# Adding up the norm sums on GpSimd, and the low parts in the three-operand form, in a four-layer model kernel

## The chip, the core and the metric

The kernel runs on one core of one Trainium2 chip, in one launch. The metric is the device time of the program in microseconds, the median of three runs before the change. A time difference of a few microseconds is a difference of a tenth of a per cent here.

## The reference, cut to what matters

A token stream of 256 tokens with 2048 features passes two layers of a first model (token mixer, then MLP, each with adaptive modulation) and two layers of a second one (an S5 layer and a FoX attention layer). Around the change only the end of each of the six branches matters:

```
y = branch(h)                                  # last step: a product with a 2048-wide weight
x = x + gate * rms_norm(y, g_post)             # for each branch
h = rms_norm(x, g_pre) * (1 + scale) + shift   # the next branch's input
```

`rms_norm` divides by the root of the mean over the 2048 features of a token. Everything is held in 32-bit floats, and products must be about that exact.

## The kernel before, in words

**Layout and slabs.** Activations lie with features on the 128 partitions: 16 blocks of 128 features by 256 tokens. Every large weight comes as slabs of 2048 x 128 (1 MB), one after the other through five buffers RAW that SyncE fills in a fixed order (`load`, L2455). One slab gives one block of 128 output features. There are 507 slabs; `slab` (L409) does 32 matmuls with each.

**High and low parts.** TensorE takes a rounded 32-bit format (fp32r). So ScalarE rounds a slab to its high part WH (`high`, L890), VectorE takes the rest WL = RAW - WH (`low`, L1566, whole slabs; `low_part`, L1562, halves of a slab), and the activations are held as high and low part beside each other. TensorE does 16 matmuls of 512 columns with WH (against high and low part), then waits for WL and does 16 of 256 columns with it. WH and WL have two buffers each. `low` counts `s_free`, on which TensorE waits before the second half and on which SyncE waits before it fills the RAW buffer again. Some slabs are used unsplit.

**Turns.** The last 16 slabs of a branch are a "turn"; there are six, i = 0 to 5 (output projection and last quarter of the down projection of layer 0: i = 0, 1; of layer 1: i = 2, 3; S5 output: i = 4; FoX output: i = 5). For output block n of a turn VectorE adds the halves of the PSUM bank to a block YT (`joined`, L1545; in turns 1 and 3 one more addition), multiplies it with the gate and x (`y_times_x`, L1634), and ScalarE squares it twice (`y_parts`, L943). These three results stand side by side in one of three buffers TS (3 x 256 columns). `y_add` (L1653) adds TS of block n to the running sum TACC. In turn 5 only the first 256 columns are there. TensorE later sums TACC and the last block's TS over the partitions with a matmul of ones (`y_sums`, L504), which waits for 14 additions of the turn. From these sums come the norm of y and that of the new x.

**Order on VectorE.** In `y_slab` (L1665) VectorE does, for each slab n of a turn: `y_times_x` of block n - 1, `y_add` of block n - 2, and `next_low` (L1574): first the modulation tile if there is one after this slab (`tile`, L1580), then the low part of the slab after. A modulation tile is 1 MB of another weight that VectorE multiplies with a broadcast row and sums; in turn 0 nearly every slab has one. In turn 3 VectorE also builds tables for the S5 layer between the slabs (names aq and abt).

**Waits on the sum.** With n >= 4, ScalarE and VectorE wait for the addition of block n - 3 before they write block n to TS again, since TS has three buffers. The engines run their instructions in the order in which the program issues them. GpSimd does nothing but four small fills at the start.

All two-operand instructions of VectorE are issued by one helper (`tt`, line L1535 in the rows), the three-operand ones by another (`stt`, L1543), matmuls by L403, ScalarE's by L888.

Of the kernel before, what the change touches and what calls it, by code (L numbers as in the profile page):

```python
# [6 lines left out]
F32 = mybir.dt.float32  # L7
F32R = mybir.dt.float32r
ALU = mybir.AluOpType
# [8 lines left out]
RING = 5  # L18
# [88 lines left out]
POS, TILE_POS, OUT_POS, LOADS = {}, {}, [], []  # L107
# [62 lines left out]
def build(nc, d, out):  # L170
    ctx = ExitStack()
    with ctx:
# [4 lines left out]
        def at(name, shape, off, dt=F32):  # L177
            return nc.alloc_sbuf_tensor_at(name, (P, *shape), dt, offset=off)
# [4 lines left out]
        def sem(name):  # L183
            return ctx.enter_context(nc.semaphore(name))
# [4 lines left out]
        RAW = [at(f"raw{i}", (KT, 128), o + 8 * kb * i) for i in range(RING)]; o += 8 * kb * RING  # L189
        WH = [at(f"wh{i}", (KT, 128), o + 8 * kb * i, F32R) for i in range(2)]; o += 16 * kb  # L190
        WL = [at(f"wl{i}", (KT, 128), o + 8 * kb * i, F32R) for i in range(2)]; o += 16 * kb
# [33 lines left out]
        TACC = at("tacc", (3, T), A0)  # L225
        TS = [at(f"ts{i}", (3, T), A0 + 3 * kb * (i + 1)) for i in range(3)]
# [95 lines left out]
        s_free = sem("s_free")  # L322
# [10 lines left out]
        s_ysq, s_yg, s_y2 = sem("s_ysq"), sem("s_yg"), sem("s_y2")  # L333
        s_t1, s_yadd = sem("s_t1"), sem("s_yadd")
# [1191 lines left out]
        def vector(e):  # L1526
# [7 lines left out]
            def tt(o_, a_, b_, op):  # L1534
                return e.tensor_tensor(o_, a_, b_, op)  # L1535
# [25 lines left out]

            def low_part(j, q):  # L1562
                w = PLACE_OF[j]
                return tt(WL[w][:, q, :], RAW[POS[j] % RING][:, q, :], WH[w][:, q, :].bitcast(F32), ALU.subtract)

            def low(j):  # L1566
                if j >= N_SLABS:
                    return
                e.wait_ge(s_hi, HI_AT[j])
                w = PLACE_OF[j]  # L1570
                tt(WL[w][:, :, :], RAW[POS[j] % RING][:, :, :], WH[w][:, :, :].bitcast(F32),
                   ALU.subtract).then_inc(s_free, 1)

            def next_low(j):  # L1574
                for t in TILES_AFTER.get(j, []):
                    tile(t)
                if j in SPLIT:
                    low(SPLIT[j])
# [55 lines left out]
            def y_times_x(i, n):  # L1634

                if i == 5:
                    return
                if i in (1, 3):
                    e.wait_ge(s_yt, 24 * (i - 1) + 32 + n + 1)
                else:  # L1640
                    e.wait_ge(s_ev, TURNS[i] + n + 1)
                if n >= 4:
                    e.wait_ge(s_yadd, 14 * i + n - 3)
                stt((TS[n % 3] if n else TACC)[:, 1, :], YT[n % 2][:, :], gate(i)[:, n:n + 1], X[:, n, :], ALU.mult,
                    ALU.mult).then_inc(s_t1, 1)
# [4 lines left out]
                    return modulation(i // 2, GATE_M if i % 2 else GATE_A)  # L1650
                return PRM[:, S5_POST:S5_POST + 16]

            def y_add(i, n):  # L1653

                q = slice(0, 1 if i == 5 else 3)
                if i == 5:
                    e.wait_ge(s_yg, 16 * i + n + 1)
                else:
                    e.wait_ge(s_y2, 16 * i + n + 1)
                    e.wait_ge(s_t1, 16 * i + n + 1)  # L1660
                if n >= 2:
                    e.wait_ge(s_yadd, 14 * i + n - 1)
                tt(TACC[:, q, :], TACC[:, q, :], TS[n % 3][:, q, :], ALU.add).then_inc(s_yadd, 1)

            def y_slab(i, n):  # L1665

                if n:
                    y_times_x(i, n - 1)
                if n >= 3:
                    y_add(i, n - 2)  # L1670
                next_low(TURNS[i] + n)
                if n == 15:
                    y_add(i, 14)

            def x_new(i, taken=None):
                y_times_x(i, 15)
# [3 lines left out]
                if i < 5:  # L1680
                    e.wait_ge(s_hi, HI_AT[TURNS[i] + 19])
                    low_part(TURNS[i] + 19, slice(0, 8))
# [33 lines left out]
                if i < 5:  # L1716
                    low_part(TURNS[i] + 19, slice(8, 16)).then_inc(s_free, 1)
                    for c in range(4):
                        normed(c)
                    for c in range(4):  # L1720
                        h_chunk_low(i, c)
                        if c == 1:
                            taken()
# [365 lines left out]
            def layer(l):  # L2089
# [17 lines left out]
                for n in range(16):  # L2107
                    if n == 0:
                        mixer_joined(l, N_IN - 1)
                        m_gated(l, 3)  # L2110
                        m_low(l, 3)
                    else:
                        joined(J_OUT[l] + n - 1, YT[(n - 1) % 2][:, :])
                    y_slab(2 * l, n)
                joined(J_OUT[l] + 15, YT[1][:, :])
                x_new(2 * l, lambda: up_taken(l, 0))
                for j in range(4):
                    for n in range(16):
                        if n:
                            up_squared(l, j, n - 1)  # L2120
                        elif j:
                            down_joined(l, j - 1, 15)
                        if n >= 2:
                            up_low(l, j, n - 2)
                        next_low(up_slab(l, j, n))
                        if l == 1:
                            s5_parameters(32 * j + n)
                    for n in range(16):
                        if n == 0:
                            up_squared(l, j, 15)  # L2130
                            up_low(l, j, 14)
                            up_low(l, j, 15)
                        else:
                            down_joined(l, j, n - 1)
                        if j == 3:
                            y_slab(2 * l + 1, n)
                        else:
                            next_low(down_slab(l, j, n))
                        if l == 1:
                            s5_parameters(32 * j + 16 + n)  # L2140
# [82 lines left out]
            def third():  # L2223
# [52 lines left out]
                for n in range(16):  # L2276
                    if n == 0:
                        joined(J_GLU + 15, ZF[1][:, :])
                        glu_gated(14)
                        glu_low(14)  # L2280
                        glu_gated(15)
                        glu_low(15)
                    else:
                        joined(J_Y2 + n - 1, YT[(n - 1) % 2][:, :], 0.25)
                    y_slab(4, n)
# [119 lines left out]
            for b in range(4):  # L2405
                e.wait_ge(s_ct0, b + 1)
                q = slice(512 * b, 512 * b + 512)
# [20 lines left out]
            for l in range(2):  # L2428
                s0 = PER_LAYER * l + SINK
                settled(ts(MINUS_SINKS[:, 16 * l:16 * l + 16], PRM[:, s0:s0 + 16], -1.0, None, ALU.mult))  # L2430
            h_chunk_low(-1, 3)
            low(RAMP)
            low(RAMP + 1)
            layer(0)
            layer(1)
            third()
            fourth()


        def source(j):  # L2440
            for l in range(2):
                if j < J_OUT[l]:
                    return d["w_in"][l, j - J_IN[l]]
                if j < J_MLP[l]:
                    return d["w_out"][l, j - J_OUT[l]]
                if j < J_MLP[l] + 128:
                    part, n = divmod(j - J_MLP[l], 32)
                    return d["w_up"][l, 16 * part + n] if n < 16 else d["w_down"][l, 16 * part + n - 16]
            for first, name in ((J_Y3, "fox_w_out"), (J_FOX, "fox_w_in"), (J_KV, "kv_w"), (J_Y2, "s5_w_out"),
                                (J_GLU, "s5_w_glu"), (J_U, "s5_w_in")):  # L2450
                if j >= first:
                    return d[name][j - first]
# [62 lines left out]
        with nc.Block() as block:  # L2515
            @block.sync
            def _(e):
                sync(e)

            @block.scalar  # L2520
            def _(e):
                scalar(e)

            @block.vector
            def _(e):
                vector(e)

            @block.tensor
            def _(e):
                tensor(e)  # L2530
# [132 lines left out]
```

## Time and profile before

| | us |
|---|---|
| median of three runs | 3237.44 (3228.82 to 3237.97) |
| the profiled execution | 3234.48 |
| its span | 3232.6 |
| TensorE busy | 3096.2 (96%) |
| VectorE busy | 2518.7 (78%) |
| ScalarE busy | 1567.5 (48%) |
| GpSimd busy | 0.2 |
| mean DMA rate | 244 GB/s |

Turn 0 lies at about 361 to 450 us of the span, turn 1 at 1087 to 1168, turn 2 at 1435 to 1518, turn 3 at 2180 to 2262, turn 4 at 2641 to 2723, turn 5 at 3134 to 3215. The busy share of the whole is an average: an engine that is 78% busy over the span can be busy all of the time in one stage and hold TensorE up there, and that is read from a stage's own rows.

In the rows, PE is TensorE, DVE is VectorE, ACT is ScalarE, POOL is GpSimd. An instruction's duration can reach a little into its successor's, so the time that one takes in a row of many is the distance between two starts, up to 0.09 us less than its duration.

### The profile page before, as it was taken

The numbers are of one execution on the slowest core, as the hardware profiler recorded it, in microseconds if no ns is written. First come the engines' busy times: TensorE is split into PE (matmuls) and PEld (weight loads), VectorE is DVE, ScalarE is ACT, GpSimd is POOL, SyncE is SP. The second block draws the span as 40 slices with busy tenths as digits, with TensorE's granted clock in tenths as the row PEclk, the third lists the DMA queues.
The fourth block names the chain that finished last, engine by engine and source line by source line (L and its number), as shares of the span: only waits on it lengthen the run. The fifth ranks groups of instructions, "written<-read, shape, count | busy, mean of one in ns | idle before, by whom it ended". The sixth has DMA issues, their size and how long they took to land. (4 is left out here: it accounts for less than half of the span.)

```text
span 3232.6 us, 49521 instructions
## 1 busy us (share of the span) xinstructions
PE 3096.2 (96%) x20336; PEld 2691.0 (83%) x20336; DVE 2518.7 (78%) x3174; ACT 1567.5 (48%) x2348; POOL 0.2 (0%) x4
## 2 busy tenths in 40 slices
PE   4899999999999999999999999999998899999998
PEld 3788778888888888888888888888887788888887
DVE  7997999798988888777987666789669677656765
ACT  2455654444444566765534444445443456434454
POOL 0000000000000000000000000000000000000000
PEclk7999999999999999999999999999999999999999
DMA  9777869988888645554687666776554553654453
GB/s 409 303 302 302 320 248 343 336 336 332 340 331 336 237 181 208 207 220 146 248 315 264 238 206 227 262 268 239 217 174 170 181 184 135 227 185 157 145 190 109
DMA packets 136978, 790.27 MB, mean 244 GB/s; under 512 B 20081, under 2 KB 38897, under 8 KB 46001
## 3 DMA queue, kind: packets, MB, share of 16 engines
q1 hardware_dynamic: 108002, 754.65, 63.2%
q10 hardware_dynamic: 28752, 32.45, 3.1%
q8 instruction: 163, 2.67, 0.3%
q14 instruction: 61, 0.50, 0.0%
HBM read 769.28 MB, written 17.76 MB: 243 GB/s over the span
## 5 line engine op out<-in xcount | busy, mean ns | idle before, releaser
L1535 DVE TENSOR_TENSOR wl<-raw,wh 128x2048 fp32r<-128x2048 f32 (+1 forms) x484 | 1097.4, 2267 | 235.0 <-ACT wh L888 234.5
L403 PE MATMUL bk<-HX,wh 128*128 128x512 f32 x4592 | 1117.1, 396 | 4.5 <-ACT wh L888 3.0
L403 PEld LDWEIGHTS bk<-HX,wh 128*128 128x128 f32 x4592 | 845.5, 189 | 178.5 <-ACT wh L888 3.6
L888 ACT ACTIVATE wh<-raw 128x2048 fp32r<-128x2048 f32 x479 | 913.7, 1908 | 31.8 <-DMA raw<-in_w_in 26.1
L403 PEld LDWEIGHTS bk<-HX,wl 128*128 128x128 f32 x4592 | 571.2, 188 | 31.3 <-DVE wl L1535 8.8
L403 PE MATMUL bk<-HX,wl 128*128 128x256 f32 x4592 | 579.1, 278 | 3.7 <-DVE wl L1535 3.7
L403 PE MATMUL bk<-hb,wh 128*128 128x512 f32 x2048 | 492.1, 392 | 2.7 <-ACT hb L888 2.4
L1543 DVE SCALAR_TENSOR_TENSOR raw<-raw,cb 128x2048 f32<-128x2048 f32 x192 | 437.5, 2285 | 14.9 <-DMA raw<-in_w_ada 14.9
L403 PEld LDWEIGHTS bk<-hb,wh 128*128 128x128 f32 x2048 | 375.3, 188 | 78.5 <-ACT hb L888 3.2
L403 PEld LDWEIGHTS bk<-hb,wl 128*128 128x128 f32 x2048 | 256.4, 189 | 12.1 <-DVE wl L1535 1.6
L403 PE MATMUL bk<-hb,wl 128*128 128x256 f32 x2048 | 259.1, 279 | 0.8 <-DVE wl L1535 0.8
L888 ACT ACTIVATE yt<-bk 128x256 f32<-128x256 f32 x160 | 61.3, 383 | 366.4 <-PE bk L403 366.4
L888 ACT ACTIVATE ur<-bk 128x256 f32<-128x256 f32 x122 | 46.8, 384 | 368.6 <-PE bk L403 361.6
L403 PE MATMUL bk<-sq,raw 128*128 128x257 f32 (+1 forms) x544 | 119.5, 380 | 2.3 <-ACT sq L888 2.3
L403 PEld LDWEIGHTS bk<-sq,raw 128*128 128x128 f32 x544 | 102.4, 189 | 18.8 <-issue 4.2
L1535 DVE TENSOR_TENSOR y<-bk,y 128x256 f32<-128x256 f32 x96 | 40.7, 424 | 75.8 <-ACT yt L888 51.7
L1535 DVE TENSOR_TENSOR ur<-bk,ur 128x256 f32<-128x256 f32 x122 | 51.3, 421 | 60.5 <-ACT ur L888 60.1
L403 PE MATMUL bk<-hf,rampw 128*128 128x256 f32 x192 | 48.3, 416 | 49.2 <-DMA rampw<-in_w_in 41.1
L403 PEld LDWEIGHTS bk<-hf,rampw 128*128 128x128 f32 x192 | 39.9, 211 | 57.5 <-DMA rampw<-in_w_in 26.0
L1535 DVE TENSOR_TENSOR tacc<-tacc,ts 128x768 f32<-128x768 f32 (+1 forms) x84 | 72.5, 863 | 1.2 <-ACT yu L888 0.6
L403 PE MATMUL bk<-ax,wh 128*128 128x512 f32 x256 | 64.8, 395 | 6.2 <-ACT wh L888 6.2
L403 PE MATMUL bk<-mx,wh 128*128 128x512 f32 x256 | 65.3, 396 | 1.2 <-DVE mx L1535 1.2
(299 smaller groups left out, 2706.1 us busy)
## 6 DMA issues: line engine op xcount, KB each, us to landing
raw<-in_w_ada SPq DMA_DIRECT2D x192, 1024.0 KB, 5.8
raw<-in_w_up SPq DMA_DIRECT2D x128, 1024.0 KB, 5.6
raw<-in_w_down SPq DMA_DIRECT2D x128, 1024.0 KB, 5.2
raw<-in_w_in SPq DMA_DIRECT2D x68, 1024.0 KB, 5.3
raw<-in_kv_w SPq DMA_DIRECT2D x33, 1024.0 KB, 4.8
raw<-in_w_out SPq DMA_DIRECT2D x32, 1024.0 KB, 4.8
raw<-in_s_w_in SPq DMA_DIRECT2D x32, 1024.0 KB, 4.8
raw<-in_fox_w_in SPq DMA_DIRECT2D x32, 1024.0 KB, 4.8
```

The source lines that it names most:

```text
L403: return e.matmul(o_, l_, r_, start=start, stop=stop, skip_group_check=True)
L888: return e.activation(o_, i_, f, **kw)
L1535: return e.tensor_tensor(o_, a_, b_, op)
L1543: return e.scalar_tensor_tensor(o_, a_, s_, b_, op0, op1, accum_out=sums)
```

## The change

The function `y_add` leaves VectorE and is issued on GpSimd, as GpSimd's only work in the program: 84 additions (14 in each of six turns; 768 columns in turns 0 to 4, 256 in turn 5), each with the same waits as before. VectorE's `y_slab` no longer has them. And every low part, which was a two-operand subtraction RAW - WH, is a three-operand instruction (RAW * 1.0) - WH: 474 whole slabs and ten halves.

```diff
             def low_part(j, q):
                 w = PLACE_OF[j]
-                return tt(WL[w][:, q, :], RAW[POS[j] % RING][:, q, :], WH[w][:, q, :].bitcast(F32), ALU.subtract)
+                return stt(WL[w][:, q, :], RAW[POS[j] % RING][:, q, :], 1.0, WH[w][:, q, :].bitcast(F32), ALU.mult,
+                           ALU.subtract)
...
-                tt(WL[w][:, :, :], RAW[POS[j] % RING][:, :, :], WH[w][:, :, :].bitcast(F32),
-                   ALU.subtract).then_inc(s_free, 1)
+                stt(WL[w][:, :, :], RAW[POS[j] % RING][:, :, :], 1.0, WH[w][:, :, :].bitcast(F32), ALU.mult,
+                    ALU.subtract).then_inc(s_free, 1)
...
             def y_slab(i, n):
 
                 if n:
                     y_times_x(i, n - 1)
-                if n >= 3:
-                    y_add(i, n - 2)
                 next_low(TURNS[i] + n)
-                if n == 15:
-                    y_add(i, 14)
...
+        def gpsimd(e):
+
+            def y_add(i, n):
+
+                q = slice(0, 1 if i == 5 else 3)
+                if i == 5:
+                    e.wait_ge(s_yg, 16 * i + n + 1)
+                else:
+                    e.wait_ge(s_y2, 16 * i + n + 1)
+                    e.wait_ge(s_t1, 16 * i + n + 1)
+                if n >= 2:
+                    e.wait_ge(s_yadd, 14 * i + n - 1)
+                e.tensor_tensor(TACC[:, q, :], TACC[:, q, :], TS[n % 3][:, q, :], ALU.add).then_inc(s_yadd, 1)
+
+            for i in range(6):
+                for n in range(1, 15):
+                    y_add(i, n)
```

On VectorE, in turn 0, two slabs stood like this before (ts is a block's three results, raw with cb a modulation tile, wl the low part, yt the block's halves joined):

```order
L1535 TENSOR_TENSOR tacc<-tacc,ts_87 128x768
L1543 SCALAR_TENSOR_TENSOR raw_54,mod<-raw_54,cb 128x2048
L1535 TENSOR_TENSOR wl_58<-raw_50,wh_56 128x2048
L1535 TENSOR_TENSOR yt_149<-bk,yt_149 128x256
L1543 SCALAR_TENSOR_TENSOR ts_86<-yt_149,mod,X 128x256
L1535 TENSOR_TENSOR tacc<-tacc,ts_88 128x768
```

and the same place now (with the buffers' numbers):

```order
L1543 SCALAR_TENSOR_TENSOR raw4_54,mod_61<-raw4_54,cb_69 128x2048
L1543 SCALAR_TENSOR_TENSOR wl1_58<-raw0_50,wh1_56 128x2048
L1535 TENSOR_TENSOR yt1_149<-bk1,yt1_149 128x256
L1543 SCALAR_TENSOR_TENSOR ts0_86<-yt1_149,mod_61,X_49 128x256
L1543 SCALAR_TENSOR_TENSOR raw1_51,mod_61<-raw1_51,cb_69 128x2048
```

The addition is gone from the row, and the low part has changed its form; nothing else has moved. GpSimd has, from the start of turn 0:

```order
L2437 TENSOR_TENSOR tacc<-tacc,ts_87 128x768 [waits s_t1,s_y2]
L2437 TENSOR_TENSOR tacc<-tacc,ts_88 128x768 [waits s_yadd,s_t1,s_y2]
L2437 TENSOR_TENSOR tacc<-tacc,ts_86 128x768 [waits s_yadd,s_t1,s_y2]
L2437 TENSOR_TENSOR tacc<-tacc,ts_87 128x768 [waits s_yadd,s_t1,s_y2]
L2437 TENSOR_TENSOR tacc<-tacc,ts_88 128x768 [waits s_yadd,s_t1,s_y2]
```

Each addition waits there for the block's product and second square, and for the addition before it; it no longer stands in front of a tile or a low part.

## Rows read from the trace of the kernel before

**Rows 1.** The page's first part: busy time, share of the span, instructions.

```profile
PE 3096.2 (96%) x20336; PEld 2691.0 (83%) x20336; DVE 2518.7 (78%) x3174; ACT 1567.5 (48%) x2348; POOL 0.2 (0%) x4
```

**Rows 2.** Waits of TensorE in turn 0, then in turn 3: total, times, longest.

```profile
PE bk L403 <- DVE wl L1535: 3.1, 9, 0.6
...
PE bk L403 <- DVE wl L1535: 0.8, 2, 0.5
```

**Rows 3.** TensorE in time order, turn 0: start, duration, what, idle before it.

```profile
366.94 2.00 PE L403 MATMUL bk<-ax,wh 128*128 128x512 f32 x8
...
383.52 2.00 PE L403 MATMUL bk<-ax,wh 128*128 128x512 f32 x8
...
444.94 2.00 PE L403 MATMUL bk<-ax,wh 128*128 128x512 f32 x8
...
450.50 1.45 PE L403 MATMUL bk<-tacc,ones 128*128 128x256 f32 x4
```

**Rows 4.** VectorE in time order, turn 0.

```profile
365.33 2.28 DVE L1543 SCALAR_TENSOR_TENSOR raw<-raw,cb 128x2048 f32<-128x2048 f32 x1
...
370.60 2.29 DVE L1543 SCALAR_TENSOR_TENSOR raw<-raw,cb 128x2048 f32<-128x2048 f32 x1
...
375.87 0.95 DVE L1535 TENSOR_TENSOR tacc<-tacc,ts 128x768 f32<-128x768 f32 x1
...
400.42 0.95 DVE L1535 TENSOR_TENSOR tacc<-tacc,ts 128x768 f32<-128x768 f32 x1
401.29 2.29 DVE L1543 SCALAR_TENSOR_TENSOR raw<-raw,cb 128x2048 f32<-128x2048 f32 x1
403.50 0.08 DVE L1543 DVE_READ_ACCUMULATOR raw<-raw,cb 128x1 f32 x1
...
443.66 0.95 DVE L1535 TENSOR_TENSOR tacc<-tacc,ts 128x768 f32<-128x768 f32 x1
...
447.59 2.04 DVE L1535 TENSOR_TENSOR tacc<-tacc,ts 128x768 f32<-128x768 f32 x2
```

**Rows 5.** ScalarE in time order, turn 0: the second square of a block.

```profile
400.34 0.49 ACT L888 ACTIVATE ts<-yt,mod 128x256 f32<-128x256 f32 x1
```

**Rows 6.** Windows: length, PE, PEld, DVE, ACT, POOL, clock, DMA share, GB/s.

```profile
40.00:90.00 50.00, 22.73 (x93) 18.90 (x93) 37.19 (x44) 3.97 (x8) 0.00 (x0) 0.73 1.01 421
...
387.30:442.90 55.60, 52.48 (x289) 43.31 (x288) 55.25 (x57) 32.28 (x46) 0.00 (x0) 1.00 0.90 343
```

**Rows 7.** TensorE in time order, turn 2.

```profile
1440.70 1.99 PE L403 MATMUL bk<-ax,wh 128*128 128x512 f32 x8
...
1451.73 1.99 PE L403 MATMUL bk<-ax,wh 128*128 128x512 f32 x8
...
1517.93 1.45 PE L403 MATMUL bk<-tacc,ones 128*128 128x256 f32 x4
```

**Rows 8.** VectorE in time order, turn 2, its last block before the sums.

```profile
1513.14 0.42 DVE L1535 TENSOR_TENSOR yt<-bk,yt 128x256 f32<-128x256 f32 x1 [1.45 <-ACT yt L888]
1513.60 0.48 DVE L1543 SCALAR_TENSOR_TENSOR ts<-yt,mod,X 128x256 f32<-128x256 f32 x1
```

**Rows 9.** VectorE in time order, turn 3.

```profile
2185.23 0.42 DVE L1535 TENSOR_TENSOR yt<-bk,yt 128x256 f32<-128x256 f32 x1
...
2233.46 0.42 DVE L1535 TENSOR_TENSOR yt<-bk,yt 128x256 f32<-128x256 f32 x1
```

**Rows 10.** All waits of VectorE in turn 3.

```profile
DVE yt L1535 <- ACT yt L888: 4.1, 6, 1.3
```

**Rows 11.** VectorE's groups by shape: form, count, busy us, mean ns, idle before.

```profile
L1535 DVE TENSOR_TENSOR wl<-raw,wh 128x2048 fp32r<-128x2048 f32 x474 | 1085.2, 2290 | 235.0 <-ACT wh L888 234.5
L1543 DVE SCALAR_TENSOR_TENSOR raw<-raw,cb 128x2048 f32<-128x2048 f32 x192 | 437.5, 2285 | 14.9 <-DMA raw<-in_w_ada 14.9
...
L1543 DVE SCALAR_TENSOR_TENSOR ts<-yt,mod,X 128x256 f32<-128x256 f32 x60 | 29.1, 485 | 2.3 <-DVE yt L1535 0.2
...
L1543 DVE SCALAR_TENSOR_TENSOR zz<-fe,zz 128x256 f32<-128x256 f32 x16 | 6.7, 420 | 0.5 <-ACT fe L888 0.5
```

More of the change, by code:

```diff
@@ L1651, in gate @@
                 return PRM[:, S5_POST:S5_POST + 16]
[L1653 to L1663, printed above, removed]
             def y_slab(i, n):
@@ L2526, in _ @@
                 vector(e)
+            @block.gpsimd
+            def _(e):
+                gpsimd(e)
             @block.tensor
```

## The prediction, made blind

> **What bounds the kernel now.** I began with the page's busy shares [rows 1]: TensorE is busy 96% of the span, VectorE 78%, GpSimd not at all. So time can fall only where TensorE runs slower than it could, and an engine with 78% on average may well be full in some stage. The change touches the six turns, so I then asked for TensorE's waits in each turn. In turns 1, 2, 4 and 5 it waits for nothing; in turn 0 it waits for the low part nine times, 3.1 us in sum, in turn 3 twice, 0.8 us [rows 2].
>
> The sum of the waits is not what turn 0 loses. Look at the pace in the time order [rows 3, 7]. Ten slabs go from 383.52 to 444.94, which is 6.14 us each. The three before them go from 366.94 to 383.52, 5.53 us each, and in turn 2, with the same shapes, two slabs take 1440.70 to 1451.73, 5.52 us each. So TensorE's own pace is 5.53 us and it runs at 6.14. (The matmuls after each wait are stretched, so part of the loss is in no wait.)
>
> VectorE's time order shows why [rows 4]. In turn 0 its rows follow each other without a gap: product, addition, modulation tile, low part, joined block. Before the additions begin one round takes 365.33 to 370.60, 5.27 us. The addition takes 400.42 to 401.29, 0.87 us on the path. Together 6.14 us, which is exactly TensorE's pace: turn 0 is bound by VectorE, at its throughput. In turn 2 the tile is missing and VectorE waits 1.45 us per slab for ScalarE [rows 8].
>
> **What the change removes.** 84 additions leave VectorE, 70 of them of 768 columns and 0.95 us [rows 4]. In turn 0 that takes VectorE's round from 6.14 to 5.27 us, under TensorE's 5.53. TensorE becomes the bound there: ten slabs take 10 x 5.53 = 55.3 instead of 61.4 us, a gain of 6.1 us. It is not 12 x 0.87 = 10.4 us (twelve additions, the first and the last in [rows 4], precede the last low part), because TensorE's own pace takes over at 5.53. What is late next is nothing of VectorE, which then has 0.26 us per slab to spare.
>
> In turn 3 the S5 tables fill VectorE: eight slabs from 2185.23 to 2233.46, 6.03 us each [rows 9], against TensorE's 5.53. The lag is mostly eaten by slack and surfaces as the 0.8 us of [rows 2]; without the additions it doesn't build up. Gain 0.8 us. In turns 1, 2, 4 and 5 the addition lies beside TensorE's work and its going is worth nothing. There the cover is VectorE's wait for ScalarE, 1.45 us per slab in turn 2.
>
> **What it adds: the additions on GpSimd.** The trace shows no such instruction. From below it could be as short as VectorE's 0.95 us, from above I take one slab, 5.53 us, where the chain of additions would itself become the bound; the value is nearer to VectorE's row, between 1 and 2 us. With no contention this is worth nothing anywhere: one addition per slab, and a block's buffer is used again three blocks later. The only hard edge is the end of a turn, where TensorE's sum waits for the 14th addition. In turn 2 the last product starts at 1513.60 and ends 0.48 us later [rows 8], and TensorE comes to the sum at 1517.93 [rows 7]: 3.8 us are there. In turn 0 the last two additions start on VectorE at 447.59 and the sum comes at 450.50 [rows 3, 4], 2.9 us for the last alone, since GpSimd does the one before it a slab earlier; and there VectorE's late joining falls away too. An addition of up to 2.5 us is covered. Cost 0, at most a few tenths per turn.
>
> **The form of the low part.** A three-operand instruction over the same 2048 columns with two inputs in SBUF takes 2285 ns, the two-operand low part 2290 [rows 11]. The tile also sums up and has a further row of 0.08 us for it [rows 4], which the low part will not have. A per-partition scalar costs something (485 against 420 ns at 256 columns [rows 11]), but here the scalar is a constant. So the cost is zero; from above 474 x 0.065 = 31 us of VectorE's busy time, of which even in turn 0 0.065 us per slab would be covered by the 0.26 to spare. From below, 5 ns per slab are nothing.
> The Trainium skill, Vector Engine (DVE) Microarchitecture Reference, section "Points that are easy to get wrong", says that this form with two SBUF sources that are not bf16 halves throughput. By that each low part would take about twice its time and the change would be a clear loss. The row of the tile, two 32-bit sources in SBUF and 2285 ns, says otherwise, and the row decides.
>
> **Transfers.** In turn 0 each slab needs two transfers of 1 MB. At 6.14 us that is 342 GB/s, and the row has 343 at a DMA share of 0.90 [rows 6]. At 5.53 us it must be 379, a share of 0.90 x 6.14 / 5.53 = 1.00. At the start of the program the queues moved 421 GB/s [rows 6], so it just fits; I count 0, at worst the 6.1 us don't come.
>
> **Sum.** 6.1 + 0.8 = 6.9 us. The profiled execution took 3234.5 us (span 3232.6), which gives 3227.6; the median of the runs is 3 us above that execution, so by the median 3230.5, and I say 3231.
>
> **Rivals.** *The shared port (slower).* If GpSimd and VectorE can't both read SBUF with two-input instructions at a time, VectorE stands still while GpSimd adds. The addition becomes ready when ScalarE's second square ends at 400.83 [rows 5], when VectorE is already in the tile from 401.29 or, without the addition, from 400.42 [rows 4], and VectorE's row in turn 0 has no gap to give. With an addition of P us VectorE's round is 5.27 + P: it is slower than before from P = 0.87 us on, and the full 6.1 us come only if P is under 0.26. For P = 1.4 turn 0 costs 12 x 0.53 = 6.4 us more than before; turn 3 has eleven additions there, 5.8 us, less VectorE's 4.1 us of waits [rows 10], 1.7; in sum +8, 3245.5. For P = 1.9 it is 12.4 + 11.3 - 4.1 = +19.6, 3257. I take 3250. For it: VectorE's rows follow on each other so densely that GpSimd must collide with something. Against it: the trace has no row of GpSimd at work, so nothing shows that either engine is held; and a form at full speed with two inputs leaves open how they are read.
> The Trainium skill, SBUF — State Buffer, section "Who interferes with whom", states just this rule: a VectorE instruction with two SBUF inputs contends with a GpSimd instruction that reads SBUF, and whoever comes second is blocked. It names no exception for the three-operand form. The GPSIMD Engine Reference, section "Elementwise — side-by-side cycle accounting", has GpSimd's addition 1.96 times as long as VectorE's, an estimate of P of about 1.9 us. No run here shows either yet.
>
> *The bound passes on (no gain).* VectorE is free but the transfers hold turn 0 at 343 GB/s, or ScalarE's chain square, rounding, copy does. Then only turn 3's 0.8 us come: 3236.6. For it the DMA share of 0.90, against it the 421 GB/s at the start.
>
> **How the numbers follow.** The forecast (no contention, 6.9 us gained) has a chance of 0.42, its own range 3226 to 3236 because the runs before spread over 9 us. The shared port has 0.38, the passed-on bound, with small mixtures near zero, 0.20. About 0.3% (9.7 us) is what a measurement tells from no change. Faster than that (under 3227.7) is only the low edge of the forecast, 0.08. Slower (over 3247.1) is the larger part of the shared port, 0.28. The rest, 0.64, is no change. The range 3226 to 3252 holds all but the top of the shared port and the lowest edge.
>
> **What the profile after would show.** Right: TensorE's slabs in turn 0 every 5.53 us, no wait for the low part there, VectorE with gaps of about 0.26 us, DMA near 379 GB/s, GpSimd's additions under 2.5 us and no VectorE row longer than before. The shared port: low parts, tiles or products in the turns longer than 2290, 2285 and 485 ns, or late after a free predecessor, in all six turns, and a pace in turn 0 over 6.14 us. The passed-on bound: ScalarE's rounding waiting for transfers, and a pace near 6.1. Wrong altogether would be low parts that are longer outside the turns, where GpSimd does nothing.

## The result, and the profile after

The changed kernel takes 3247.4 us (median of seven runs, 3244.14 to 3251.66) against 3237.44 us in as many runs of the kernel before (3228.82 to 3244.57). The ratio is 1.0036 with a 95% interval of 1.0021 to 1.0051: slower by 0.36%, which is 12 us (the two medians lie 10 us apart), where I had forecast 7 us faster. The forecast was wrong; the rival of the shared port said 3245 to 3257.

The profiled execution has a span of 3249.8 us. Its page gives GpSimd work to do, and it is more than was taken from VectorE:

```profile
PE 3103.3 (95%) x20336; PEld 2695.1 (83%) x20336; DVE 2489.4 (77%) x3090; ACT 1568.4 (48%) x2348; POOL 249.4 (8%) x88
```

VectorE is rid of 84 additions but only of 29 us of busy time against [rows 1], not of the 72.5 us that these took on it. Instructions that became longer take back 35 us; the remaining 8 us or so are no work at all, since a duration reaches a little into its successor's and is counted there once. The groups by shape tell which became longer (line, form, count, busy us, mean ns, idle before):

```profile
L1543 DVE SCALAR_TENSOR_TENSOR wl<-raw,wh 128x2048 fp32r<-128x2048 f32 x474 | 1103.5, 2328 | 265.3 <-ACT wh L888 264.6
L1543 DVE SCALAR_TENSOR_TENSOR raw<-raw,cb 128x2048 f32<-128x2048 f32 x192 | 437.4, 2285 | 13.9 <-DMA raw<-in_w_ada 13.8
...
L1535 DVE TENSOR_TENSOR aq<-ah,bq 128x768 f32<-128x768 f32 x32 | 35.8, 1160 | 1.3 <-DMA ah<-at_keep 1.3
...
L1535 DVE TENSOR_TENSOR yt<-y,yt 128x256 f32<-128x256 f32 x32 | 21.6, 675 | 1.1
```

The low parts have grown by 18 us, one addition of blocks (yt<-y,yt) by 8 us and the table products (aq) by 7 us; two single instructions of turn 0 make up the other 2 us. A mean of 2328 ns instead of 2290 looks like a small, even slowing. It is not. In time order it is eleven instructions of 3.94 us, all in turn 0, and 463 that are as before (11 x 1.65 us is the whole difference of 18 us). Two slabs of turn 0 on VectorE, then the same stretch on GpSimd:

```profile
391.98 0.48 DVE L1543 SCALAR_TENSOR_TENSOR ts<-yt,mod,X 128x256 f32<-128x256 f32 x1
392.38 2.28 DVE L1543 SCALAR_TENSOR_TENSOR raw<-raw,cb 128x2048 f32<-128x2048 f32 x1
394.59 0.08 DVE L1543 DVE_READ_ACCUMULATOR raw<-raw,cb 128x1 f32 x1
394.59 3.94 DVE L1543 SCALAR_TENSOR_TENSOR wl<-raw,wh 128x2048 fp32r<-128x2048 f32 x1
398.46 0.41 DVE L1535 TENSOR_TENSOR yt<-bk,yt 128x256 f32<-128x256 f32 x1
398.90 0.48 DVE L1543 SCALAR_TENSOR_TENSOR ts<-yt,mod,X 128x256 f32<-128x256 f32 x1
399.31 2.28 DVE L1543 SCALAR_TENSOR_TENSOR raw<-raw,cb 128x2048 f32<-128x2048 f32 x1
401.52 0.08 DVE L1543 DVE_READ_ACCUMULATOR raw<-raw,cb 128x1 f32 x1
401.52 3.94 DVE L1543 SCALAR_TENSOR_TENSOR wl<-raw,wh 128x2048 fp32r<-128x2048 f32 x1
```

```profile
392.88 3.51 POOL L2437 TENSOR_TENSOR tacc<-tacc,ts 128x768 f32<-128x768 f32 x1 [3.42 <-ACT ts L888]
399.80 3.50 POOL L2437 TENSOR_TENSOR tacc<-tacc,ts 128x768 f32<-128x768 f32 x1 [3.42 <-ACT ts L888]
...
459.21 1.86 POOL L2437 TENSOR_TENSOR tacc<-tacc,ts 128x768 f32<-128x768 f32 x1 [0.42 <-DVE ts L1543]
```

Read the two together. The addition becomes ready at 392.88, while VectorE is in a tile. It cannot do its work at once: it takes 3.5 us, where the last of the turn, with VectorE idle beside it, takes 1.86. The 1.7 us that are left to the tile's end at 394.59 are its wait, which the trace counts as its duration. Then the addition has the port, and now the low part stands still: it takes 3.94 us instead of 2.29, 1.65 us more. Each instruction that waits looks busy; in these rows a stall at the port shows as a long instruction, never as idle time.

VectorE's round is now 399.31 - 392.38 = 6.93 us, against 5.27 + 0.87 = 6.14 before [rows 4], and TensorE follows it (start, duration, what, idle before):

```profile
393.66 2.00 PE L403 MATMUL bk<-ax,wh 128*128 128x512 f32 x8
395.49 2.00 PE L403 MATMUL bk<-mx,wh 128*128 128x512 f32 x8
398.59 1.21 PE L403 MATMUL bk<-ax,wl 128*128 128x256 f32 x8 [1.10 <-DVE wl L1543]
399.64 1.10 PE L403 MATMUL bk<-mx,wl 128*128 128x256 f32 x8
400.58 2.00 PE L403 MATMUL bk<-ax,wh 128*128 128x512 f32 x8
```

Its waits for the low part in turn 0 went from the 3.1 us of [rows 2] to this:

```profile
PE bk L403 <- DVE wl L1543: 12.8, 12, 1.2
```

To compare turns, take the time from the start of block 0's product on VectorE (of its square on ScalarE in turn 5) to TensorE's sum of TACC. It is the same to 0.1 us where nothing changes, in turns 1, 4 and 5. Turn 2 has 80.3 to 81.7 us in all kernels, whatever they do there. Turn 3 has 82.2 to 85.1 us in the five kernels whose turn 3 is that of before (before and four of the experiments below). In us:

| | turn 0 | turn 1 | turn 2 | turn 3 | turn 4 | turn 5 |
|---|---|---|---|---|---|---|
| before | 85.57 | 81.19 | 80.68 | 82.21 | 81.10 | 80.51 |
| changed | 95.69 | 81.18 | 81.70 | 86.45 | 81.10 | 80.50 |

Turn 0 costs 10.1 us. Turn 3 shows 4.2 us in this pair, but the three kernels with whole additions on GpSimd there have 86.0 to 86.5 us against the 82.2 to 85.1, so its own loss is known only as 1 to 4 us. Together that is 11 to 14 us, inside the interval of the ratio (7 to 17 us). The 17 us between the two profiled spans contain 3 us from stretches that the change doesn't touch.

Turn 3 shows the other side of the same thing. VectorE, then GpSimd:

```profile
2218.72 0.42 DVE L1535 TENSOR_TENSOR yt<-bk,yt 128x256 f32<-128x256 f32 x1 [0.91 <-ACT yt L888]
2219.18 1.06 DVE L1535 TENSOR_TENSOR yt<-y,yt 128x256 f32<-128x256 f32 x1
...
2220.68 2.28 DVE L1543 SCALAR_TENSOR_TENSOR wl<-raw,wh 128x2048 fp32r<-128x2048 f32 x1
2222.88 3.48 DVE L1535 TENSOR_TENSOR aq<-ah,bq 128x768 f32<-128x768 f32 x2
```

```profile
2218.10 1.86 POOL L2437 TENSOR_TENSOR tacc<-tacc,ts 128x768 f32<-128x768 f32 x1 [6.55 <-ACT ts L888]
2221.28 3.41 POOL L2437 TENSOR_TENSOR tacc<-tacc,ts 128x768 f32<-128x768 f32 x1 [1.32 <-ACT ts L888]
```

From 2218.10 to 2219.96 GpSimd adds. The joining of a block, with one input in PSUM and one in SBUF, runs in the middle of it at its usual 0.42 us. The next instruction has both inputs in SBUF and takes 1.06 instead of 0.43 us; it ends 0.28 us after the addition. The next addition becomes ready at 2221.28, in the low part, and waits for its end; then the pair of table products takes 3.48 instead of 1.82 us, again 1.66 more. Later in the turn, where no table products follow, the stall is 1.2 us (1.62 instead of 0.42 us, four times), since the joining hides a part of the addition.

In turns 1, 2, 4 and 5 no instruction of VectorE is longer. There GpSimd is the one that waits: in turn 2 an addition starts at 1468.44, in the low part from 1467.70 to 1469.99, and takes 3.27 us; it then works while VectorE waits for ScalarE.

### The profile page after: what moved, and what is told of

It is laid out like the page before. It is cut to its first block and busy times, and to the rows that moved or that the text cites. A ratio compares the mean times of both kernels' runs of the same rounds, so it can differ in the third digit from the quotient of the medians.

```text
span 3249.8 us, 49523 instructions
## 1 busy us (share of the span) xinstructions
PE 3103.3 (95%) x20336; PEld 2695.1 (83%) x20336; DVE 2489.4 (77%) x3090; ACT 1568.4 (48%) x2348; POOL 249.4 (8%) x88
## 5 line engine op out<-in xcount | busy, mean ns | idle before, releaser
L1543 DVE SCALAR_TENSOR_TENSOR wl<-raw,wh 128x2048 fp32r<-128x2048 f32 (+1 forms) x484 | 1115.7, 2305 | 265.3 <-ACT wh L888 264.6
L2437 POOL TENSOR_TENSOR tacc<-tacc,ts 128x768 f32<-128x768 f32 (+1 forms) x84 | 249.2, 2966 | 2980.2 <-ACT ts L888 2517.1
L1535 DVE TENSOR_TENSOR yt<-bk,yt 128x256 f32<-128x256 f32 x64 | 26.9, 421 | 61.7 <-ACT yt L888 61.7
```

Of the source, the lines that this page charges most:

```text
L1543: return e.scalar_tensor_tensor(o_, a_, s_, b_, op0, op1, accum_out=sums)
L2437: e.tensor_tensor(TACC[:, q, :], TACC[:, q, :], TS[n % 3][:, q, :], ALU.add).then_inc(s_yadd, 1)
```

## The experiments

The theory after these rows is that a GpSimd instruction that reads SBUF and a VectorE instruction with two inputs in SBUF exclude each other for whole instructions, and that the one that waits gets the port when the other's instruction ends. The rivals are that the three-operand form is to blame, that the loss sits in later sums at the turns' ends, or that something other than VectorE holds turn 0.

**form_only.** The three-operand low parts alone, with the additions left on VectorE.

```diff
-                tt(WL[w][:, :, :], RAW[...][:, :, :], WH[w][:, :, :].bitcast(F32), ALU.subtract)
+                stt(WL[w][:, :, :], RAW[...][:, :, :], 1.0, WH[w][:, :, :].bitcast(F32), ALU.mult, ALU.subtract)
```

> The low parts in the three-operand form, the additions left on VectorE. Theory (GpSimd's additions and VectorE's two-input instructions exclude each other, whatever the form): no change, ratio 1.000, whole low parts 2.29 us everywhere, turn 0 at 6.14 us per slab. Rival (the three-operand form is what costs): the whole loss is here, about +11 us, low parts longer than 2.29 us.

Ratio 0.9996 (0.9987 to 1.0005), turn 0 85.57 us:

```profile
L1543 DVE SCALAR_TENSOR_TENSOR wl<-raw,wh 128x2048 fp32r<-128x2048 f32 x474 | 1085.1, 2289 | 234.4 <-ACT wh L888 234.0
```

2289 against 2290 ns [rows 11]: the form by itself costs nothing, and does not lose half its rate.

**gp_two_operand.** The additions alone on GpSimd: the changed kernel with the low parts' `stt` put back to `tt`.

> The additions on GpSimd, the low parts in the old two-operand form. Theory: as the changed kernel, ratio about 1.0036 (1.002 to 1.005), low parts in turn 0 about 3.94 us and its slabs 6.93 us apart. Rival one (the three-operand form is the one that collides): 3230 us, low parts 2.29 us, turn 0 at 5.53 us. Rival two (the two-operand form collides worse, which the change wanted to avoid): slower than the changed kernel, above 3250 us, with low parts over 3.94 us or low parts of other turns lengthened too.

Ratio 1.0032 (1.0020 to 1.0045), turn 0 95.68 us, turn 3 86.14. In turn 0:

```profile
400.94 3.94 DVE L1535 TENSOR_TENSOR wl<-raw,wh 128x2048 fp32r<-128x2048 f32 x1
```

The same 3.94 us in both forms. The two-operand form collides neither more nor less, so the three-operand form buys nothing. Both rivals about the form fall.

**no_add.** GpSimd's instruction is kept with all its waits, but cut to one column; the sums are left out:

```diff
-                e.tensor_tensor(TACC[:, q, :], TACC[:, q, :], TS[n % 3][:, q, :], ALU.add).then_inc(s_yadd, 1)
+                e.tensor_tensor(TACC[:, 0, 0:1], TACC[:, 0, 0:1], TS[n % 3][:, 0, 0:1], ALU.add).then_inc(s_yadd, 1)
```

> Each GpSimd addition is cut to one column of one of its three parts, with all its waits and counts; the running sums are left out. Theory: with the additions' time on the shared port gone, VectorE's round in turn 0 is 5.27 us and TensorE's pace of 5.53 us takes over; turn 0 gains 6.1 us and turn 3 0.8 us over before, 3230 us, ratio 0.998, low parts 2.29 us. Rival (the bound passes on to the transfers, 343 GB/s in turn 0): 3236.6 us, turn 0 stays near 6.1 us per slab, ScalarE's rounding waits for transfers.

Ratio 0.9978 (0.9969 to 0.9987), 7 us faster than before. Turn 0 takes 79.17 us, 6.4 less than before. Stretch 390 to 440 us (length, PE, PEld, DVE, ACT, POOL busy, clock, DMA share, GB/s):

```profile
390.00:440.00 50.00, 50.00 (x291) 43.99 (x290) 46.16 (x46) 32.56 (x50) 10.42 (x10) 1.00 0.99 397
```

TensorE is full and the queues follow to a share of 0.99. So the part of the prediction that reads turn 0 as bound by VectorE, and prices its relief at 6.1 us, was right, and the rival of the passed-on bound falls. (GpSimd's 10.42 us there are ten tiny instructions of 0.2 to 2.3 us, most of which end with the tile or low part in which they become ready; the low parts keep their 2.29 us.)

**write_only.** The addition becomes a fill of the same columns, a write without a read; the sums are left out.

```diff
-                e.tensor_tensor(TACC[:, q, :], TACC[:, q, :], TS[n % 3][:, q, :], ALU.add).then_inc(s_yadd, 1)
+                e.memset(TACC[:, q, :], 1.0).then_inc(s_yadd, 1)
```

> Each GpSimd addition is replaced by a fill of the same 768 or 256 columns (a write with no read); the running sums are left out. If only reads exclude each other: low parts 2.29 us, turn 0 at 5.53 us, 3230 us. If any access of GpSimd to SBUF does: low parts in turn 0 longer by the fill's duration and a pace of 5.27 us plus that.

Ratio 0.9984 (0.9974 to 0.9994), turn 0 79.17 us, low parts 2289 ns. A fill in the middle of a tile, GpSimd and then VectorE:

```profile
403.44 0.74 POOL L2437 MEMSET tacc<- 128x768 f32 x1 [4.21 <-ACT ts L888]
```

```profile
401.99 2.29 DVE L1543 SCALAR_TENSOR_TENSOR raw<-raw,cb 128x2048 f32<-128x2048 f32 x1
```

Neither is longer: all fills of GpSimd take 0.74 us in the mean. So a write alone does not exclude, and the read does.

**one_input.** A copy of TS into TACC instead of the addition: one read. The sums are left out.

```diff
-                e.tensor_tensor(TACC[:, q, :], TACC[:, q, :], TS[n % 3][:, q, :], ALU.add).then_inc(s_yadd, 1)
+                e.tensor_copy(TACC[:, q, :], TS[n % 3][:, q, :]).then_inc(s_yadd, 1)
```

> Each GpSimd addition is replaced by a copy of the block's three results into the running sum, one input instead of two; the running sums are left out. If any read of GpSimd excludes VectorE's two-input instructions: low parts in turn 0 lengthened by about the copy's own duration, say 0.7 to 1.3 us, a pace of 6.0 to 6.6 us, 3228 to 3240 us, about the time of before. If only two-input reads do: low parts 2.29 us, pace 5.53 us, ratio 0.998.

Ratio 0.9992 (0.9982 to 1.0001). In turn 0, then GpSimd's copies there and the last one, which has no VectorE beside it:

```profile
402.59 2.90 DVE L1543 SCALAR_TENSOR_TENSOR wl<-raw,wh 128x2048 fp32r<-128x2048 f32 x1
```

```profile
400.86 2.50 POOL L2437 COPY tacc<-ts 128x768 f32<-128x768 f32 x1 [3.39 <-ACT ts L888]
...
445.54 0.83 POOL L2437 COPY tacc<-ts 128x768 f32<-128x768 f32 x1 [0.91 <-ACT ts L888]
```

One read excludes as well. The stall is 0.61 us for a copy of 0.83 us, just under my range of 0.7 to 1.3. Rounds come every 5.88 us, which is 5.27 + 0.61 and just under my 6.0 to 6.6, and turn 0 takes 83.12 us, 2.45 less than before: this stall is on the gaining side of 0.87 us. (A copy is less work than the addition, so this shows where the break-even lies, not a way to get the sums. In the time of the whole kernel it can't be told from no change.)

**gp_quiet and gp_full.** The additions of only some turns on GpSimd, the others on VectorE.

```diff
+ON_GPSIMD = (1, 2, 4, 5)        # gp_full: (0, 3)
...
+                if n >= 3 and i not in ON_GPSIMD:
+                    y_add(i, n - 2)
...
-            for i in range(6):
+            for i in ON_GPSIMD:
```

> As the changed kernel, but the additions of turns 0 and 3 are back on VectorE; 56 additions stay on GpSimd, in turns 1, 2, 4 and 5. Theory (the port stalls cost time only where VectorE has no slack, turns 0 and 3): as before, ratio 1.000 within 0.001, turn 0 at 6.14 us per slab. Rival (the loss is spread over all turns, or sits in the waits for later sums at their ends): ratio 1.002 or more.

> The counterpart: only the 28 additions of turns 0 and 3 on GpSimd. Theory: the whole loss, ratio 1.0036 (1.002 to 1.005): 10 us in turn 0 at 6.93 us per slab, 4 us in turn 3. Rival (loss spread over all turns): a third of it, ratio 1.0012.

gp_quiet: 0.9998 (0.9990 to 1.0007), turns 1, 2, 4, 5 as before. gp_full: 1.0039 (1.0026 to 1.0051), turn 0 95.66, turn 3 86.04. The 28 additions of turns 0 and 3 are the whole loss; the 56 others, 161 us of GpSimd's time, cost nothing and bring nothing. In gp_quiet GpSimd alone is held up: its additions take 3.16 us in the mean, and no VectorE instruction of the turns is longer. No run has the additions of turn 0 alone on GpSimd, so what turn 3 adds is not separated from its scatter.

**gp_split.** Each addition in three pieces of 256 columns.

```diff
-                e.tensor_tensor(TACC[:, q, :], TACC[:, q, :], TS[n % 3][:, q, :], ALU.add).then_inc(s_yadd, 1)
+                for c in range(q.stop):
+                    last = e.tensor_tensor(TACC[:, c, :], TACC[:, c, :], TS[n % 3][:, c, :], ALU.add)
+                last.then_inc(s_yadd, 1)
```

> The changed kernel, with each GpSimd addition of 768 columns issued as three of 256 (0.74 us each when alone, against 1.86 us). Theory (the port is held for a whole instruction and handed over at its end to whoever waits): every stall of VectorE becomes short, 0.5 us or so, and there are more of them: the low part about 2.8 us instead of 3.94, the product or the tile lengthened as well, and one piece partly hidden behind the joining of a block, which has one input in SBUF; turn 0 at 6.4 to 6.8 us per slab, between before (6.14) and the changed kernel (6.93), ratio about 1.002. Rival (access is shared element by element, and only the amount counts): low parts stay near 3.94 us and the pace at 6.93.

Ratio 1.0018 (1.0009 to 1.0027), turn 0 89.19 us, turn 3 85.35. One round of VectorE:

```profile
399.80 0.41 DVE L1535 TENSOR_TENSOR yt<-bk,yt 128x256 f32<-128x256 f32 x1
400.25 0.51 DVE L1543 SCALAR_TENSOR_TENSOR ts<-yt,mod,X 128x256 f32<-128x256 f32 x1
400.67 2.83 DVE L1543 SCALAR_TENSOR_TENSOR raw<-raw,cb 128x2048 f32<-128x2048 f32 x1
403.43 0.08 DVE L1543 DVE_READ_ACCUMULATOR raw<-raw,cb 128x1 f32 x1
403.43 2.82 DVE L1543 SCALAR_TENSOR_TENSOR wl<-raw,wh 128x2048 fp32r<-128x2048 f32 x1
406.17 0.41 DVE L1535 TENSOR_TENSOR yt<-bk,yt 128x256 f32<-128x256 f32 x1
```

There are three short handovers instead of one long one: tile and low part each stand still for 0.54 us, and the third piece is hidden behind the joining and leaves 0.03 us on the product. The round is 6.37 us. The port passes from one engine to the other at the end of every instruction, not element by element. In pieces the total stall is less (1.1 us against 1.65), because one piece falls where VectorE does not need the port. It still loses against 0.87 us on VectorE itself.

**pe_share and pe_three.** If neither VectorE nor GpSimd is to add, TensorE can: some of turn 0's blocks are summed over the partitions at once, into the two banks in which the sums end.

```diff
+BY_TENSOR = (3, 6, 9, 12)        # pe_three: (4, 8, 11)
...
+                mm(yy[:, 0:T], ONES[:, 0:128], TS[n % 3][:, 0, :], first, False)
+                mm(xy[:, :], ONES[:, 0:128], TS[n % 3][:, 1:3, :].rearrange("p a t -> p (a t)"), first,
+                   False).then_inc(s_yadd, 1)
...
-                if n >= 3:
+                if n >= 3 and not (i == 0 and n - 2 in BY_TENSOR):
                     y_add(i, n - 2)
```

> The kernel before, with four of turn 0's fourteen additions (blocks 3, 6, 9, 12) taken off VectorE and done by TensorE: it sums these blocks over the partitions with ones straight into the two PSUM banks in which the turn's sums end. VectorE's round is then 5.27 + 0.87 x 0.7 = 5.9 us on average, TensorE's 5.53 + 1.3 x 0.3 = 5.9 us, against 6.14: a gain of 0.25 us for twelve slabs, 3 us, ratio 0.999. If VectorE's bound in turn 0 is as I read it, the turn ends 2 to 4 us earlier; if TensorE's extra matmuls are on the path instead (5 us for four blocks), it ends later or the same.

> As pe_share with three blocks (4, 8, 11) instead of four. The four blocks cost TensorE 1.23 us each, 4.9 us of the 6.4 us that its waits in turn 0 are worth. With three VectorE saves 3 x 0.87 = 2.6 us and TensorE has 6.4 - 3.7 = 2.7 us left to gain, so the turn should end 2.6 us earlier than before (4 blocks: 0.9), ratio 0.999.

Ratios 0.9994 (0.9986 to 1.0003) and 0.9995 (0.9986 to 1.0004), no difference that can be told. Turn 0 took 84.65 and 84.60 us, 0.9 and 1.0 less than before, where I expected 3 and 2.6. For four blocks the error is plain: each costs TensorE 1.2 us (6.38 + 5.89 us for the slab with the sum and the one after it, against 2 x 5.53), and 6.4 - 4.9 leaves 1.5, not 3. For three blocks, 6.4 - 3.7 = 2.7 us were to be had, and 1.0 of them TensorE still loses in the two slabs ahead of block 4, before the first relief comes:

```profile
383.45 2.00 PE L404 MATMUL bk<-ax,wh 128*128 128x512 f32 x8
...
389.41 2.00 PE L404 MATMUL bk<-ax,wh 128*128 128x512 f32 x8
...
393.56 1.21 PE L404 MATMUL bk<-ax,wl 128*128 128x256 f32 x8 [0.31 <-DVE wl L1550]
...
395.55 1.45 PE L404 MATMUL bk<-ts,ones 128*128 128x256 f32 x4
```

These slabs take 5.96 and 6.14 us instead of 5.53: I had averaged over the turn where the order counts. The last 0.7 us I have not traced. No version that computes the sums is faster than the kernel before by more than the measurement can tell.

## Why the prediction was wrong, point by point

- **What bounds turn 0: right.** I had a gain of 6.1 us there once VectorE is rid of the additions' time; no_add gave 6.4 us, and a ratio of 0.9978 where 6.9 us would be 0.9979.
- **Turn 3: not contradicted, but not shown.** I forecast 0.8 us and no_add shows 1.1, less than the 3 us by which this turn scatters. In the changed kernel the turn lost 4.2 us (3.8 in gp_full and 3.9 in gp_two_operand), where the rival's sum at P = 1.65 gives 11 x 0.78 - 4.1 = 4.5. That this fits is partly luck: the sum has eleven stalls of 1.65 us, while the rows have thirteen, five of 0.64, four of 1.2 and four of 1.66 us, 14.6 us in all.
- **The additions on GpSimd at cost 0: this step failed.** "With no contention this is worth nothing anywhere" was a condition that I took without a row. The runs show a stall of 1.65 us per slab in turn 0 and a round of 6.93 us, in place of 0 and 5.27 us. The duration itself, 1.86 us alone, lay in the 1 to 2 us that I named, and the turns' ends were covered as said.
- **The form of the low part: right.** form_only shows no effect. The Trainium skill's sentence on the halved throughput of this form (Vector Engine (DVE) Microarchitecture Reference, "Points that are easy to get wrong") does not hold here: 2289 ns against 2290 for the two-operand form.
- **The transfers: right.** A share of 0.99 and 397 GB/s in no_add, without holding TensorE up.
- **The chances.** The rival had the mechanism, turn 0 as the place, the break-even at a stall of 0.87 us, and the time. Its sign of longer VectorE rows in all six turns did not come: they are longer in turns 0 and 3 only. Its round of 5.27 + P is a little high too, 7.13 us at P = 1.86 against 6.93. The rule is that of the Trainium skill (SBUF — State Buffer, "Who interferes with whom"), and every run here agrees with it, the exception for instructions that only write included (write_only: low parts of 2289 ns). The estimate of P from the Trainium skill (GPSIMD Engine Reference, "Elementwise — side-by-side cycle accounting") was 1.9 us; the row has 1.86. I gave the rival 0.38 against 0.42 because the trace of before had no row of GpSimd at work. But a trace without a row speaks for neither side, and a stated rule then should have weighed more.

The time difference is made of 10.1 us in turn 0 (6.93 against 6.14 us per slab), 1 to 4 us in turn 3, and nothing that can be told in the other four.

## What to carry to other kernels

Moving an elementwise instruction that reads SBUF from a full VectorE to GpSimd was not a relief here but a swap. VectorE stood still for nearly the time that GpSimd took (1.65 of 1.86 us), and GpSimd took twice as long as VectorE itself (1.86 against 0.95 us). The break-even is a stall as long as the instruction's own time on VectorE, 0.87 us here. By these rows such a move can pay only where the VectorE instructions beside it have at most one input in SBUF, or where VectorE has idle time, and in the four turns where it had some it was worth nothing. When a trace shows an instruction longer than its group's usual duration, look at what the other engine does in the same microseconds before reading it as a slower form.

## What the runs showed of the hardware that I had not expected

- The engine that waits gets the port at the next instruction's end, even when the other engine's next instruction is queued right behind. In turn 0 eleven of the fourteen additions got in between a tile and a low part, and the twelfth between a tile and a small addition (16 columns, 1.70 instead of 0.17 us). The short accumulator row of 0.08 us behind each tile is not what lets GpSimd in: in turn 3 it got in between a low part and the table products, where there is no such row. In the turns of the changed kernel, gp_two_operand, gp_full and gp_quiet no addition waited longer than to the end of the VectorE instruction in which it became ready.
- VectorE's stall is a little less than the duration that the profile gives GpSimd's instruction when it runs alone: 1.65 of 1.86 us for 768 columns added, 0.61 of 0.83 copied, 0.54 of 0.74 for 256 columns added. About 0.2 us of each GpSimd instruction is not held against VectorE.
- A fill of 768 columns on GpSimd (0.74 us) runs beside VectorE's instructions with two inputs in SBUF and neither is longer; so does VectorE's joining from PSUM beside a GpSimd addition.
